# Fetching the first token tile's expert outputs by ScalarE's queue, and splitting two weight quarters of the second column block earlier, in a two-layer kernel on one core

## The reference, cut to what matters

```python
    out = jnp.zeros((n_tok, d)).at[buf_tok].add(yb * buf_w[:, None])   # two experts' outputs per token
    ...
    x = x + out                                # end of the first block's mixture
    x = rms_norm(x, final_norm_w)              # the first block's output
    ...
    h = rms_norm_2(x, attn_norm_g) @ w_in      # the second block's input projection
```

## Time and profile before

| what | us |
|---|---|
| median of 3 runs | 2467.88 (2467.82 to 2468.67) |
| the profiled execution's own time | 2466.94 |
| its span, first to last instruction | 2465.7 |
| TensorE busy | 2249.9 (91%) |
| VectorE busy | 936.1 (38%) |
| ScalarE busy | 701.5 (28%) |
| GpSimd busy | 585.5 (24%) |

### The profile page before, as it was taken

The page is one execution under the profiler, slowest core; times in us unless marked ns, Lnnn a source line. Parts: engine busy times, 40 slices in busy tenths (PEclk is TensorE's granted clock), DMA queues, the critical chain, the costliest instruction groups (busy, mean ns, idle before and its releaser), DMA issues.

```text
span 2465.7 us, 32513 instructions
## 1 busy us (share of the span) xinstructions
PE 2249.9 (91%) x13122; PEld 1659.2 (67%) x13122; DVE 936.1 (38%) x1817; ACT 701.5 (28%) x1379; POOL 585.5 (24%) x685
## 2 busy tenths in 40 slices
PE   7999999999999989988888778788879999999999
PEld 5776888988888565554444444444447857888887
DVE  5677677776322241110000000000127575542441
ACT  4545556565221010000000000000014475331330
POOL 4443577775100111111111111111104160000000
PEclk9999999999999999999999999999999999999999
DMA  7322243443436489999999999999983212122220
GB/s 188 99 79 73 86 143 97 122 135 129 180 114 263 157 345 425 425 427 426 426 426 426 426 426 427 427 426 426 427 322 133 86 36 69 69 103 103 103 102 36
DMA packets 149593, 575.46 MB, mean 233 GB/s; under 512 B 14972, under 2 KB 75928, under 8 KB 124736
## 3 DMA queue, kind: packets, MB, share of 16 engines
q1 hardware_dynamic: 127728, 534.77, 54.7%
q0 software_dynamic: 16288, 28.98, 3.5%
q10 hardware_dynamic: 5424, 9.58, 1.5%
HBM read 562.69 MB, written 31.52 MB: 241 GB/s over the span
## 4 chain that ended last, share of the span: by engine, by line
PE 59%; DMA 28%; DVE 6%; ACT 3%; issue 3%; POOL 2%; ACTq 0%; DVEq 0%; SPq 0%; POOLq 0%
PE ps L689 14%; PE ps L691 13%; PE ps L690 13%; DMA ringx<-in_w_expert_gate 7%; DMA ringx<-in_w_expert_up 6%; PE ps L1051 6%; DMA ring<-in_w_expert_up 4%; DMA ring<-in_w_expert_gate 4%; PE ps L1081 3%; PE ps L953 2%; PE ps L682 2%; DMA ringx<-in_w_expert_down 2%; DMA ringy<-in_w_expert_gate 2%; DMA ringy<-in_w_expert_up 1%; PE ps L794 1%
## 5 line engine op out<-in xcount | busy, mean ns | idle before, releaser
L2312 DVE TENSOR_TENSOR hid<-ps,sg 128x256 f32<-128x256 f32 x64 | 27.2, 425 | 823.6 <-issue 808.3
L689 PE MATMUL ps<-hTh,hb 128*128 128x512 f32 x576 | 237.0, 411 | 3.0 <-DVE ringr L1883 3.0
L1051 PE MATMUL ps<-ringx,gxT 128*64 128x256 f32 x1664 | 200.4, 392 | 40.6 <-DMA ringx<-in_w_expert_up 25.4
L691 PE MATMUL ps<-hTh,ringr 128*128 128x512 f32 x576 | 226.1, 393 | 0.0
L690 PE MATMUL ps<-hTl,hb 128*128 128x512 f32 x576 | 225.1, 391 | 0.0
L1674 ACT COPY ys<-ps 128x512 f32<-128x512 f32 x64 | 37.5, 586 | 621.8 <-PE ps L1081 621.8
L1051 PEld LDWEIGHTS ps<-ringx,gxT 128*64 128x64 f32 x1664 | 135.0, 135 | 113.8 <-issue 66.0
L2734 POOL DMA_INDIRECT gx<-h2d,rows x64 | 65.7, 1027 | 507.1 <-PE ps L682 441.7
L1883 DVE TENSOR_TENSOR ringr<-ring,hb 128x1024 fp32r<-128x1024 f32 x112 | 147.8, 1321 | 89.8 <-ACT hb L1400 89.1
L1051 PE MATMUL ps<-ring,gxT 128*64 128x256 f32 x1216 | 145.7, 390 | 29.5 <-DMA ring<-in_w_expert_up 18.7
L1051 PE MATMUL ps<-ringy,gxT 128*64 128x256 f32 x1216 | 145.3, 390 | 27.6 <-DMA ringy<-in_w_expert_up 17.5
(11 more groups left out here) (458 smaller groups left out, 4641.5 us busy)
## 6 DMA issues: line engine op xcount, KB each, us to landing
ringx<-in_w_expert_gate SPq DMA_DIRECT2D x26, 2048.0 KB, 45.6
ringx<-in_w_expert_up SPq DMA_DIRECT2D x26, 2048.0 KB, 46.0
ringx<-in_w_expert_down SPq DMA_DIRECT2D x25, 2048.0 KB, 46.0
ring<-in_w_expert_down SPq DMA_DIRECT2D x19, 2048.0 KB, 46.1
ring<-in_w_expert_gate SPq DMA_DIRECT2D x19, 2048.0 KB, 45.6
ring<-in_w_expert_up SPq DMA_DIRECT2D x19, 2048.0 KB, 46.1
ringy<-in_w_expert_down SPq DMA_DIRECT2D x19, 2048.0 KB, 46.2
ringy<-in_w_expert_gate SPq DMA_DIRECT2D x19, 2048.0 KB, 45.6
```

Of the source, the lines that this page charges most:

```text
L689: pe.matmul(o, lh, rh, start=start and n == 0, stop=False)
L691: m = pe.matmul(o, ll, rh, start=False, stop=stop and n == len(ks_) - 1)
L1051: m = pe.matmul(b[c * 64:c * 64 + 64, 0:256].rearrange("p (n j) -> p n j", j=2), gxTs[e % 2][:, k % 4, k // 4 * 64:k // 4 * 64 + 64], w4[: ...
```

## The change

Three edits. SP no longer fetches the first tile's two outputs; ScalarE issues these DMAs at the head of `act_combine`, before its first weight quarters. VectorE forms quarter 3's low part behind the sums of tile 1, not between the low part and the sums. In the second column block, `act_hi2(4)` and `act_hi2(5)` come behind the first and the second of the four squares (were behind the third and the fourth), `dve_lo2(4)` comes behind the second of the four norm products (was behind the fourth), and `dve_lo2(5)` ahead of the extraction (was behind it).

```diff
     def sp_second():
-        for tt in range(NT):
+        for tt in range(1, NT):
             for k in range(2):
                 sp.dma_start(Ys[k][:, tt, :], ybuf[k * S + tt * 128:k * S + tt * 128 + 128, :]).then_inc(s[f"cy{tt}"], 16)
...
     def act_combine():
+        for k in range(2):
+            a.dma_start(Ys[k][:, 0, :], ybuf[k * S:k * S + 128, :]).then_inc(s["cy0"], 16)
         for b in range(4):
             act_hi2(b)
...
                              accum_out=st[:, 72 + q:73 + q]).then_inc(s["q5"], 1)
-            if 4 <= b < 20:
+                if q < 2:
+                    act_hi2(4 + q)
+            elif b < 20:
                 act_hi2(b)
...
-            if tt == 0:
-                dve_lo2(2)
+            if tt < 2:
+                dve_lo2(2 + tt)
             dve_rows_low(tt)
-            if tt == 0:
-                dve_lo2(3)
...
             if c == 0:
                 dve_last_norm(q)
-            if 4 <= 4 * c + q + 1 < 20:
+                if q in (1, 3):
+                    dve_lo2(4 + q // 2)
+            elif 5 < 4 * c + q + 1 < 20:
                 dve_lo2(4 * c + q + 1)
```

## The result

| what | before | changed |
|---|---|---|
| median of 12 runs, us | 2469.82 (2466.56 to 2472.98) | 2465.40 (2463.10 to 2469.79) |
| profiled execution's own time | 2466.94 | 2463.10 |
| its span | 2465.7 | 2461.8 |

The ratio of the changed kernel to the one before is 0.9984, 95% interval 0.9977 to 0.9992: 4.0 us less, between 2.0 and 5.7. I had forecast 5.9 less and 2462.0 us, with a range up to 2465.2; the measured median lies 0.2 us above it. Of the 3.4 us between forecast and median, 1.9 us are the level of the kernel before, which came out at 2469.82 in twelve runs and 2467.88 in the first three. The other 1.5 us are the gain: the two medians differ by 4.4 us, not by 5.9.

The account below looks back on a forecast made before the run. TensorE was held up at the seam by tile 0's late pair, a half-clock stretch and waits for quarters 4 and 5. 2.0 + 1.7 + 2.2 = 5.9 us off 2467.88 gave 2462.0, range 2459.8 to 2465.2.

Parts of the forecast that it names:

- First edit, 2.0 forecast: Behind the branch, ScalarE's queue fetches tile 0's pair earlier, so TensorE's first real transpose starts 2.0 us sooner.
- The rival of no effect: ScalarE's DMAs behind the branch start no sooner than SP's did; only 2.2 us are left, 2465.7; chance 0.06.
- its rival: Tile 0's pair lands late, in 7.2 us; gain 3.2 to 4.9 us, 2463.0 to 2464.7; chance 0.10.
- The rival on the shared DMA engines: Tile 0's pair is served among SP's six transfers, landing near 1844.7; slower, 2473.8; chance 0.03.
- The clock, 1.7: First column block: TensorE's clock stays up, so 3.41 us of matmuls at half clock go; 1.7 us, between 0 and 1.7.
- Second edit, 0 beyond cover: VectorE's quarter 3 behind tile 1's sums avoids a stall of 0 to 0.4 us; counted as 0 gain.
- Third edit, 2.2: Second column block: earlier quarters 4 and 5 remove TensorE's waits, third block starts 2.2 us earlier, between 1.3 and 2.65.
- So the extraction stays at 1873.41. This margin is 0.8 us.: Second column block: fourth square ends at 1871.4, GpSimd's fourth root began at 1872.24, so the extraction is not delayed.
- the third of the signs of being wrong: The prediction is wrong if GpSimd's roots end later in relation to TensorE's last product.
- The level, 2462.0: Whole kernel: forecast median, 2467.88 for the kernel before less 5.9 us.

Follow-up runs that it names:

- the last experiment: On the changed kernel: three norm products, quarter 4's low part, fourth product, quarter 5's; GpSimd's roots ahead of its DMA issues; 28 idle transposes; median 2461.91, ratio 0.9976.

## Why the prediction was right and wrong

**First edit, 2.0 forecast: right in its mechanism, a little high.** The profile gave 13.46 - 11.95 = 1.51. The other five kernels with 36 idle transposes and the early pair have A of 11.62, 11.59, 12.09, 11.18 and 11.53, in the mean of six 11.66, so 1.8 less than before. The transposes were named as what comes next, and they were. Their time varied from 5.75 to 6.26 us with the moment at which the clock rose, which the old kernel hid behind the sums. The rival of no effect fell. The pair was late by half of what its rival said, 6.2 us where 5.0 and 7.2 stood, and the transposes hid it. The rival on the shared DMA engines fell too: SP issued its first transfer at 1831.27, while the pair was still under way, and the pair landed at 1834.5 all the same, some 4 us before the 1838.8 at which a loss would begin:

```profile
1831.27 3.14 SPq L652 DMA_DIRECT2D Y<-ybuf  x6
```

That sharing made the 6.2 us is not shown: in the last experiment SP issued only 3.6 us behind ScalarE's first issue, and the pair took 6.2 us there too.

**The clock, 1.7: right.** B of the first two edits alone is 1.57 shorter than before. The clock did not fall again. It fell in the two kernels in which TensorE idles 2.00 and 2.12 us ahead of its first real transposes, and in none of the nine in which that idle time is 0.62 us or less, though the gap of 0.96 us behind them is there in all eleven. In these eleven only transposes ran while the clock rose. So the rule of "TensorE: Matmul & The Clock Gate", "Part 4: PE-mode transpose", in the Trainium skill, that a transpose does not count as activity, by which the clock would have fallen, is not borne out here.

**Second edit, 0 beyond cover: right**, 0.2 measured.

**Third edit, 2.2: wrong.** The step that failed is "So the extraction stays at 1873.41. This margin is 0.8 us." It counted when GpSimd's inputs would be ready, and gave its instructions the durations of the old place. Its own times had the two meet: they put the third norm product behind quarter 4's low part, from 1867.7, and tile 0's roots began at 1867.81 in the old trace. Tile 0's roots took 1.03 + 1.45 us instead of 0.22 + 0.57. Of these 1.7 us, 0.35 came back in the instruction behind them, 0.21 instead of 0.56. From the start of tile 0's root to the extraction it was 6.9 us (1864.91 to 1871.83) where it had been 5.6 (1867.81 to 1873.41), 1.3 more, and GpSimd idled nowhere in it. The last root ended 7.2 us behind the start of the first block's last matmul (1864.62 to 1871.79), where it had been 5.9 (1867.51 to 1873.37): the third of the signs of being wrong that the prediction names. The gap was 1.61 instead of 0.15, 1.46 more; 1.3 are the roots, and 0.1 is VectorE's saving behind the extraction, which was 1.20 and not 1.32. With 1.46 taken off, the 2.2 become 0.74; measured were 0.71 and 0.74. The old trace held both kinds, in GpSimd's timeline:

```profile
1862.80 0.97 POOL L2615 TENSOR_SCALAR st<-st 128x1 f32<-128x1 f32 x1 [3.79 <-ACT Y L1700]
1863.85 1.46 POOL L2616 TENSOR_TENSOR st<-st,consts 128x1 f32<-128x1 f32 x1
...
1872.54 0.56 POOL L2616 TENSOR_TENSOR st<-st,consts 128x1 f32<-128x1 f32 x1
```

The first two lie beside VectorE's norm products, the last, its first instruction being's of 0.22 us, while VectorE is idle. The prediction used the start time of one of them and never compared their durations.

The measured sum of parts is 1.8 + 1.6 + 0.7, 4.1 us, against the ratio's 4.0. A margin of 0.8 us was counted as if safe. With the roots' two speeds in the sum, the forecast would have been 4.4 us and the chances nearer to no change.

**The level, 2462.0: off by the kernel before.** Its three runs happened to lie within 0.9 us; twelve spread over 6.4 us. I took the three for the kernel's level. In the runs of the changed kernel the mean granted clock goes from 0.992 to 0.997; what sets that from run to run was not tried.

## What to carry to other kernels

When work is moved on VectorE, look at what GpSimd does in the new place, and at the old trace for how long the same GpSimd instruction takes beside VectorE and alone; a margin counted in ready times does not hold if the durations change. Work that only keeps TensorE awake becomes the bound once what it covered is faster, so size it again with each such change. Where single runs scatter more than the change is worth, measure between two events of one trace.

## What the hardware showed that I had not expected

GpSimd's instruction on one element per partition took 0.22 us with VectorE idle and 1.03 us beside a 128x1024 product; the second, 0.57 and 1.45. In the changed kernel the first began at 1864.91 and ended at 1865.94, just behind the first of two products (1864.57, 1.28 us); the second began at 1866.02 and ended at 1867.47 behind the other's end near 1867.04. That looks like waiting for whole instructions rather than sharing. The Trainium skill has this in "SBUF — State Buffer", under "Who interferes with whom": a VectorE instruction with two inputs in SBUF contends with a GpSimd instruction that reads SBUF, and whoever comes second waits for the other to end. The traces agree: the first instruction ended 0.1 us behind the product, the second 0.4 us behind, each within 0.2 us of the product's end plus the time that it takes alone (0.22 and 0.57). Which resource it is, the runs do not say.

Behind the branch ScalarE was ready within 0.3 us of the landing, SP only 2.7 to 3.9 and TensorE 3.6 to 4.1 us after it, in all twelve traces. What lets one engine start sooner was not tried.
